# The gate product: expert tiles outside and tokens inside, or the other way round

## The reference

```
s1, i1 = lax.top_k(s[:, :, 0], K)              # K = 16; 8 heads; 128 keys a side
s2, i2 = lax.top_k(s[:, :, 1], K)
...
cand_i = (i1[..., :, None] * PEER_N_KEYS + i2[..., None, :]).reshape(T, PEER_HEADS, K * K)
top_s, top_pos = lax.top_k(cand_s, K)
expert_idx = jnp.take_along_axis(cand_i, top_pos, axis=-1)
gates = jax.nn.softmax(top_s, axis=-1)
ub = jnp.take(u, eb, axis=0)
act = jax.nn.gelu(jnp.einsum('thkd,td->thk', ub, xb), approximate=False)
vb = jnp.take(v, eb, axis=0)
return jnp.einsum('thk,thkd->td', gb * act, vb)
```

## Time and profile before

| | us |
|---|---|
| median of 3 runs | 2997.28 (2995.55 to 2999.19) |
| span of the profiled execution | 2998.2 |
| TensorE matmul busy | 2734.9 (91%) |
| TensorE weight load busy | 2417.8 (81%) |
| VectorE busy | 1819.1 (61%) |
| ScalarE busy | 1457.1 (49%) |
| first gate stage, first product to end of the last | 610.61 to 750.27 |
| second gate stage | 1752.84 to 1892.60 |

### The profile page before, as it was taken

The page is one execution under the profiler, slowest core; times in us unless marked ns, Lnnn a source line. Parts: engine busy times, 40 slices in busy tenths (PEclk is TensorE's granted clock), DMA queues, the critical chain, the costliest instruction groups (busy, mean ns, idle before and its releaser), DMA issues.

```text
span 2998.2 us, 47842 instructions
## 1 busy us (share of the span) xinstructions
PE 2734.9 (91%) x16426; PEld 2417.8 (81%) x16430; DVE 1819.1 (61%) x3134; ACT 1457.1 (49%) x2435; POOL 13.8 (0%) x29
## 2 busy tenths in 40 slices
PE   8889999977999997889999976899997998998898
PEld 6689999965888876579999965788876986866797
DVE  3456786499555553245778479655555656454564
ACT  4334444487454543334444477445444544553543
POOL 0000000000000000000000000000000000000000
PEclk9899999977999998789999987999998998998999
DMA  6245555500555553145555520455555554533454
GB/s 202 71 141 183 182 182 173 192 14 0 186 192 193 192 178 103 34 136 179 180 184 169 182 69 0 137 195 192 194 182 164 182 189 142 170 109 113 146 181 149
DMA packets 123982, 446.85 MB, mean 149 GB/s; under 512 B 14280, under 2 KB 14920, under 8 KB 123648
## 3 DMA queue, kind: packets, MB, share of 16 engines
q1 hardware_dynamic: 119808, 434.16, 44.0%
q0 software_dynamic: 2608, 9.08, 1.0%
q10 hardware_dynamic: 1488, 2.59, 0.2%
HBM read 444.74 MB, written 1.05 MB: 149 GB/s over the span
## 4 chain that ended last, share of the span: by engine, by line
PE 79%; DVE 13%; issue 4%; ACT 3%; DVEq 1%; DMA 0%; ACTq 0%
PE ps L621 38%; PE ps L593 12%; PE ps L599 12%; PE ps L596 12%; DVE SC L1750 3%; DVE big L1758 3%; DVE w_lo L337 1%; DVE SC L1400 1%; DVE X L1407 1%; DVEq L1750 1%; PE ps L571 1%; PE ps L818 1%; DVE tops L1694 1%; DVE big L1407 1%; DVE x_lo L1454 1%
## 5 line engine op out<-in xcount | busy, mean ns | idle before, releaser
L337 DVE TENSOR_TENSOR w_lo<-ring,w_hi 128x1024 fp32r<-128x1024 f32 (+1 forms) x808 | 986.2, 1221 | 917.8 <-ACT w_hi L330 907.0
L330 ACT CAST w_hi<-ring 128x1024 fp32r<-128x1024 f32 (+1 forms) x808 | 845.2, 1047 | 1115.8 <-PE ps L621 582.3
L593 PE MATMUL ps<-x_hi,w_hi 128*128 128x256 f32 x3136 | 775.4, 285 | 8.7 <-DVE x_lo L1459 4.4
L596 PE MATMUL ps<-x_lo,w_hi 128*128 128x256 f32 x3136 | 773.3, 284 | 0.0
L593 PEld LDWEIGHTS ps<-x_hi,w_hi 128*128 128x128 f32 x3136 | 605.0, 193 | 11.5 <-issue 10.4
L596 PEld LDWEIGHTS ps<-x_lo,w_hi 128*128 128x128 f32 x3136 | 605.3, 193 | 0.0
L599 PE MATMUL ps<-x_hi,w_lo 128*128 128x256 f32 x3136 | 443.3, 284 | 4.0 <-DVE w_lo L337 4.0
L621 PE MATMUL ps<-w_hi,x_hi 128*128 128x512 f32 x1488 | 417.8, 400 | 26.1 <-DVE x_lo L1454 12.6
L599 PEld LDWEIGHTS ps<-x_hi,w_lo 128*128 128x128 f32 x3136 | 405.7, 193 | 7.7 <-DVE w_lo L337 7.7
L621 PE MATMUL ps<-w_hi,x_lo 128*128 128x512 f32 x1488 | 409.8, 394 | 0.0
L621 PE MATMUL ps<-w_lo,x_hi 128*128 128x512 f32 x1488 | 407.9, 393 | 0.3 <-DVE w_lo L337 0.3
(11 more groups left out here) (221 smaller groups left out, 1512.5 us busy)
## 6 DMA issues: line engine op xcount, KB each, us to landing
ring<-in_u SPq DMA_DIRECT2D x256, 512.0 KB, 3.3
ring<-in_v SPq DMA_DIRECT2D x256, 512.0 KB, 3.2
ring<-in_ffn_in SPq DMA_DIRECT2D x88, 512.0 KB, 3.3
ring<-in_ffn_out SPq DMA_DIRECT2D x44, 512.0 KB, 3.3
ring<-in_wq SPq DMA_DIRECT2D x32, 512.0 KB, 3.3
ring<-in_ple_gate SPq DMA_DIRECT2D x16, 512.0 KB, 3.3
SC<-in_rows POOLq DMA_DIRECT2D x11, 512.0 KB, 4.4
ring<-in_a_qk SPq DMA_DIRECT2D x8, 512.0 KB, 4.5
```

The costliest lines, as they stand in the source:

```text
L330: nc.scalar.copy(part(w_hi, i)[:, used(name)], tile(i)[:, used(name)]).then_inc(tiles_hi, 1)
L337: nc.vector.tensor_tensor(part(w_lo, i)[:, at], tile(i)[:, at], part(w_hi, i)[:, at], ALU.subtract).then_inc(tiles_split, 1)
L593: mm = nc.tensor.matmul(bank(s)[:, 0:T], hi[:, k, :], x_hi[:, k, :], start=(k == 0), stop=False)
L596: nc.tensor.matmul(bank(s)[:, 0:T], hi[:, k, :], x_lo[:, k, :], start=False, stop=False)
```

## The change

Both views of the product's operands are turned: the activations and the PSUM bank are now walked with the expert tile (e) outside and the four tokens (t) inside. In memory nothing moves; each of the 512 products of an instruction is the same as before and goes to the same place.

```diff
@@ -1754,8 +1754,8 @@
                 def apply_gates(k, turns=0):
 
                     slot_here(dve, base + k, turns)
-                    h = expert_tokens[:, ds(turns * 16 + 4 * k, 4), :]
-                    free(V.tensor_tensor(h, h, bank(base + k).rearrange("p (t e) -> p t e", t=4), ALU.mult),
+                    h = expert_tokens[:, ds(turns * 16 + 4 * k, 4), :].rearrange("p t e -> p e t")
+                    free(V.tensor_tensor(h, h, bank(base + k).rearrange("p (t e) -> p e t", t=4), ALU.mult),
                          base + k)
 
                 for k in range(4):
```

## The result

The changed kernel takes 2923.42 us (median of 4 runs, 2920.57 to 2924.67) against 2996.5 for the kernel before (4 runs): 0.976 of it, 95% interval 0.9748 to 0.9772, or 73 us less. The case named as likeliest came true for the product, but the forecast of 2934 is 10.6 us too high, and the range's low end of 2925 lies 1.6 us above the median.

A forecast was written before the change was run, and what follows sets the result against it. VectorE was taken to bound each layer's gate stage. With 64 periods of 1.73 us per layer, 64.7 us are saved together: 2998.2 - 64.7 - 0.9 = 2932.6, plus 1.4 for waiting, said as 2934 us; range 2925 to 3004.

The forecast's parts named there:

- The case named as likeliest: Gate-stage product at or under about 0.75 us, kernel at 2927 to 2943 us; chance 0.50.
- VectorE bounds the gate stage, and what the product gives back comes out of the end: Gate stage of each layer: VectorE busy 139 of 140 us, so shorter products end it earlier until another engine is late.
- The new walk costs nothing extra, 682 ns: VectorE product in the gate stage: falls from 1.289 us to 682 ns, the time of 512 elements without strides.
- the row that made a strided SBUF read nearly free: A VectorE instruction reading 16 elements 516 bytes apart takes 180 ns against 174 contiguous, so the stride costs 6 ns.
- ScalarE is next, at 1.69 us: Gate stage: ScalarE's unhindered first turn took 6.77 us for four periods, 1.69 each, against VectorE's 1.63 after the change.
- The same share of time at the low clock afterwards, 1.73 us: Gate stage: TensorE stays at 1.2 GHz 0.44 of the time, 0.44 x 1.78 + 0.56 x 1.69 = 1.73 us per period.
- 1.4 us for engines waiting on one another: Gate stage: a guessed addition for three engines within 0.15 us of each other per period, sometimes waiting on one another.
- What follows the stage is not touched: The v stage behind each gate stage waits only for that stage's end and keeps its length.
- the case in which TensorE is never slow: Gate stage: TensorE always at the high clock, 64 x 1.69 saves 34.9 us per layer and gives 2927.5 us.
- The rivals: Gate-stage product: PSUM stride costs the whole old SBUF penalty (0.18, 2997 us), half (0.13, 2959), or more (0.19, 3075 at twice).

## Why the prediction was right or wrong

- *VectorE bounds the gate stage, and what the product gives back comes out of the end.* Right.
- *The new walk costs nothing extra, 682 ns.* Right in size (685), and in part by luck. Short inner runs are free, as assumed, and so is the strided PSUM read. But the evidence for reads was the row that made a strided SBUF read nearly free, and that is not so (362 ns for 512 elements); nor is the write the larger part in what a period pays. It did no harm, since the new walk has no strided SBUF read of single words and PSUM shows no such cost.
- *ScalarE is next, at 1.69 us.* Right, by the trace and by the run that takes work from it.
- *The same share of time at the low clock afterwards, 1.73 us.* This is the step that failed: the term for the period, 1.73 us in the sum, measured 1.69. I held TensorE's clock constant while I gave it the same work in three quarters of the time. It stayed at 2.4 GHz after the opening (a mean of 0.99 over each stage instead of 0.78 and 0.81). The term was worth 2.6 us per layer in the sum, 5.1 in all. Whether a low clock would have cost the changed kernel anything stays untried: half the matmuls at 1.2 GHz cost nothing, but the full work at 1.2 GHz (1.78 us a group for its loads) did not come up.
- *1.4 us for engines waiting on one another.* Nothing of the sort is in the trace; ScalarE never waits. The comparisons went from 331 to 342 ns, the distances from 389 to 396 and the relu from 614 to 624, and ScalarE's pace is the 1.69 us of before all the same.
- *What follows the stage is not touched.* Wrong by 1.4 and 1.6 us: the v stage used to open at a mean clock of 0.83 (second layer 0.79) over its first 8 us and now opens at 1.00.

```profile
752.00:760.00 8.00, 8.00 (x30) 6.51 (x31) 4.53 (x6) 3.62 (x6) 0.00 (x0) 0.83 0.59 172
```

```profile
717.70:725.70 8.00, 8.00 (x35) 6.64 (x36) 5.58 (x7) 4.29 (x7) 0.00 (x0) 1.00 0.68 199
```

The first of these is of the kernel before, the second of the changed one. All twelve traces agree on the price: a v stage that opens at 1.00 takes 350.5 us, and one that opens at 0.76 to 0.83 takes 351.9 to 352.4. But the clock of the gate stage doesn't decide how the next one opens. With half the matmuls, at 0.50 throughout, one v stage opened at 1.00 and one at 0.76; with the write strided, at 1.00 after the start, both opened at 0.79. Why both opened at 1.00 in the changed kernel stays open.

Against the forecast saving of 63.3 us (64.7 less 1.4), measured in the two gate stages and behind them were 71.4. The stages gave 68.4, which is 3.7 more than 64.7: the clock term of 5.1, less some 1.4 that my sum without it had too much. The 1.4 us of waiting that did not come and the 3.0 of the v stages make the rest. That leaves about 2 us to the 73 of the medians, and 0.8 us more lie in the starting point, 2997.3 in the forecast and 2996.5 with the fourth run; together these are the 10.6. The 2 us are not settled: the kernel before scatters between 2989 and 3002 us in these runs, the changed one between 2920 and 2928.

- *The range.* Its low end allowed 2.5 us below the case in which TensorE is never slow. That case, 2927.5, was nearly what happened, and neither the v stages nor the scatter of before were in it.
- *The rivals.* The penalty changed sides in none of the ways thought of: VectorE's PSUM read shows no cost at a stride of 512 bytes.

## What to carry to other kernels

When a VectorE instruction takes twice what its element count gives in its neighbours' rows, look at the innermost step of its SBUF operands: here two neighbouring words were enough, and moving the stride to the PSUM operand, at 512 bytes a step, cost nothing. Compare the starts of consecutive instructions too, and not durations alone. When a bound goes, read the next engine's pace where nothing held it (its first turn), and ask of each quantity that depends on load, TensorE's clock first, what the shorter period makes of it rather than carry it over. Before work is given to an idle engine, time one instruction of it there.

## What was not expected of the hardware

- Strided SBUF words, 1024 bytes apart, cost VectorE 0.71 ns each when read and 0.80 when written, 1.19 when both; in pairs of neighbours 0.07. These are durations (1044, 1090, 1289 and 720 against 682 ns); until the next instruction starts, the read costs more than the write (0.956 against 0.885 us, 0.60 without).
- A strided PSUM read at 512 bytes costs VectorE nothing measurable (685 against 683 ns).
- GpSimd's comparison of 128 elements takes 600 ns back to back, where VectorE's comes every 0.26 us; while it runs all the time, VectorE's comparisons go from 342 to 373 ns.
- With half of its matmuls TensorE ran a whole stage at 1.2 GHz, with 39 us of 60 busy, at no cost to the kernel (2923.14 against 2923.42 us).
- A v stage takes 350.5 us when it opens at 2.4 GHz and about 352.1 when its first 8 us have a mean clock of about 0.8.
